# Recurrent layer: gate products in three rounded passes, the convolution's sum and the decay's square in banks, the gate weights' rest on GpSimd

## What is computed

```
xb, g = split(h @ w_in)                          # h: 512 x 1024, w_in: 1024 x 3072
xc = conv_b + conv_w[3]*xb + sum over k<3 of conv_w[k] * (xb delayed by 3-k tokens)
r = sigmoid(xc_head @ gate_a_w[head] + gate_a_b) # per head, 128 x 128
i = sigmoid(xc_head @ gate_x_w[head] + gate_x_b)
a = exp(-8 * r * softplus(-lam));  mult = sqrt(1 - a*a)
h_t = a_t * h_(t-1) + mult_t * i_t * xc_t        # scan over the tokens
y = h * silu(g);  out = y @ w_out                # w_out: 1536 x 1024
```

## Time and profile before

| | |
|---|---|
| median of 3 runs | 1899.43 us (1898.32 to 1899.71) |
| profiled execution | 1898.7 us, of which the span of its instructions is 1897.0 us |
| TensorE busy | 1859.6 us of the span (98%) |
| GpSimd, VectorE, ScalarE busy | 1323.5 us (70%), 863.7 us (46%), 476.6 us (25%) |
| mean granted TensorE clock | 0.995 of full |
| stretch 389 to 552 us, which holds the changed stage | TensorE busy 162.1 of 163.0 us |

### The profile page before, as it was taken

How to read it: one execution, slowest core, us unless ns; L and a number is a source line. 1 busy time by engine, 2 the same in 40 slices (tenths; PEclk the granted TensorE clock), 3 DMA queues, 4 the chain that set the end, 5 groups by cost and what they waited for, 6 DMA issues and landing times.

```text
span 1897.0 us, 25309 instructions
## 1 busy us (share of the span) xinstructions
PE 1859.6 (98%) x8668; PEld 1512.5 (80%) x8668; DVE 863.7 (46%) x1465; ACT 476.6 (25%) x868; POOL 1323.5 (70%) x1303
## 2 busy tenths in 40 slices
PE   7999999999999999999999999999999999999998
PEld 6888888877778788888888767798876768888886
DVE  5166663168973422233047655644354172222621
ACT  3111111146651111111033244343323231111001
POOL 7766666767677777776677887672772667777765
PEclk9999999999999999999999999999999989999999
DMA  4222224232222322232232211100331222223231
GB/s 180 92 88 89 90 91 149 90 122 75 74 83 102 112 108 88 96 128 92 83 111 100 75 59 45 45 23 1 134 111 45 70 75 97 102 88 105 95 107 71
DMA packets 25128, 170.45 MB, mean 90 GB/s; under 512 B 2784, under 2 KB 2912, under 8 KB 6624
## 3 DMA queue, kind: packets, MB, share of 16 engines
q1 hardware_dynamic: 23328, 159.92, 23.9%
q10 hardware_dynamic: 1728, 9.58, 1.4%
HBM read 167.39 MB, written 2.10 MB: 89 GB/s over the span
## 4 chain that ended last, share of the span: by engine, by line
PE 93%; DVE 3%; ACT 1%; POOL 1%; issue 1%; DMA 0%; DVEq 0%; ACTq 0%; POOLq 0%
PE bank L399 20%; PE bank L401 20%; PE bank L400 20%; PE bank L437 2%; PE bank L439 2%; PE bank L438 2%; PE bank L1219 2%; PE bank L1218 2%; PE bank L1220 2%; PE bank L786 1%; PE bank L1605 1%; PE bank L1607 1%; PE bank L1606 1%; PE bank L2264 1%; PE bank L2248 1%; PE bank L1843 1%
## 5 line engine op out<-in xcount | busy, mean ns | idle before, releaser
L303 POOL TENSOR_TENSOR weights_lo<-raw_weights,weights_hi 128x512 fp32r<-128x512 f32 (+3 forms) x560 | 759.0, 1356 | 53.1 <-ACT weights_hi L322 7.2
L301 POOL TENSOR_SCALAR weights_hi<-raw_weights 128x512 fp32r<-128x512 f32 (+4 forms) x536 | 363.7, 679 | 396.5 <-PE bank L401 281.3
L399 PE MATMUL bank<-x_hi,weights_hi 128*128 128x512 f32 x1264 | 500.3, 396 | 0.2
L401 PE MATMUL bank<-x_lo,weights_hi 128*128 128x512 f32 x1264 | 492.2, 389 | 0.0
L400 PE MATMUL bank<-x_hi,weights_lo 128*128 128x512 f32 x1264 | 491.9, 389 | 0.0
L399 PEld LDWEIGHTS bank<-x_hi,weights_hi 128*128 128x128 f32 x1264 | 237.4, 188 | 52.8 <-issue 4.3
L400 PEld LDWEIGHTS bank<-x_hi,weights_lo 128*128 128x128 f32 x1264 | 237.4, 188 | 51.9 <-issue 3.6
L401 PEld LDWEIGHTS bank<-x_lo,weights_hi 128*128 128x128 f32 x1264 | 237.3, 188 | 49.8
L1046 DVE TENSOR_TENSOR temps<-bank,rms_rows 128x512 f32<-128x512 f32 x44 | 30.4, 690 | 185.7 <-PE bank L401 185.7
L1036 ACT ACTIVATE ffn_y_hi<-temps 128x512 f32 (+1 forms) x44 | 27.8, 633 | 228.8 <-DVE temps L1049 228.8
L437 PE MATMUL bank<-weights_hi,x_hi 128*128 128x512 f32 x160 | 64.4, 402 | 11.2 <-DVE x_lo L527 10.7
(11 more groups left out here) (453 smaller groups left out, 3247.1 us busy)
## 6 DMA issues: line engine op xcount, KB each, us to landing
raw_weights<-in_ffn_up SPq DMA_DIRECT2D x44, 1024.0 KB, 4.8
raw_weights<-in_a_ug SPq DMA_DIRECT2D x16, 1024.0 KB, 4.7
raw_weights<-in_b_in SPq DMA_DIRECT2D x12, 1024.0 KB, 4.8
raw_weights<-in_ffn_down SPq DMA_DIRECT2D x8, 1408.0 KB, 6.0
raw_weights<-in_ffn_down SPq DMA_DIRECT2D x11, 1024.0 KB, 4.8
raw_weights<-in_a_out SPq DMA_DIRECT2D x8, 1024.0 KB, 4.7
raw_weights<-in_a_v SPq DMA_DIRECT2D x7, 1024.0 KB, 4.8
raw_weights<-in_b_out SPq DMA_DIRECT2D x8, 768.0 KB, 4.2
```

Of the source, the lines that this page charges most:

```text
L301: nc.gpsimd.tensor_scalar(hi, raw, 1.0, 0.0, ALU.mult, ALU.add).then_inc(S("units_hi"), 1)
L303: nc.gpsimd.tensor_tensor(lo, raw, hi.bitcast(F32), ALU.subtract).then_inc(units_ready, 1)
L399: nc.tensor.matmul(ps, wh, xh[:, k, :], start=k == 0, stop=False)
L401: last = nc.tensor.matmul(ps, wh, xl[:, k, :], start=False, stop=k == last_k)
```

## The change

The gate products become three matmuls each, as in `feature_tile`, from rounded halves. ScalarE's copy of the gate matrices is now the rounded half (`b_gate_hi`); GpSimd makes its rest (`b_gate_lo`, the new function `pool_gates_low`, called behind unit 1 of each following round, and once behind the last round). The convolution's sum stays in its bank; ScalarE copies it rounded to `b_xc_hi`, and VectorE makes the rest `b_xc_lo` (`conv_low`). The square of the decay goes to bank 4 in place of a buffer, so `gates` also waits for `b_m2`, the last read of that bank.

```diff
--- before.py
+++ after.py
@@ -153,9 +153,9 @@
     _members("sq", ("gl", 2 * GH), ("go", GH)) + [("go_act_diags", 2)], _members("sums", ("gl", GH), ("go", GH)), *(_members(kind, ("gl", GH), ("go", GH)) for kind in ("diags", "spread", "scaled")),
     *([(f"b_{b}", n * KB), (f"g_{g}", n * 3 * GH)] for b, g, n in (("xb", "xb", 1), ("xc0", "c0", 1), ("taps", "taps", 2), ("xc", "conv", 1))),
     *(_members(kind, ("fx", FOXH * TOK), ("ma", MH * TOK)) for kind in ("s", "nm", "e", "p", "t", "pt")),
-    [("row_sel", 3), ("f_rows", 1), ("gb_split", 4), ("go_with_q", TOK)], [("row_ones", 3), ("mask_b", 2), ("f_queries", 2)],
+    [("b_xc_lo", KB), ("row_sel", 3), ("f_rows", 1), ("gb_split", 4), ("go_with_q", TOK)], [("b_xc_hi", KB), ("row_ones", 3), ("mask_b", 2), ("f_queries", 2)],
     [("beta_tanh", 1), ("a_exp", 1), ("rows_exp", 1)],
-    [("causal", 2), ("masks", 26)], [("b_thg", KB), ("g_th", 4 * GH)], [("b_sg", KB), ("fx_r", FOXH * TOK)],
+    [("b_gates_lo", KB), ("causal", 2), ("masks", 26)], [("b_thg", KB), ("g_th", 4 * GH)], [("b_sg", KB), ("fx_r", FOXH * TOK)],
     [("raw_first0", 16), ("mem_in", 32)], [("raw_first1", 16), ("stored", 16 * KD)],
     [("fx_o", FOXH), ("ma_o", 2 * MH)], [("fx_hi", FOXH // 2), ("ma_hi", 2 * MH)], [("fx_lo", FOXH // 2), ("ma_lo", 2 * MH)],
 ]
@@ -257,9 +257,11 @@
         B_YH = place("b_y_hi", YAT, [KB, SEQ], F32R)
         B_YL = place("b_y_lo", YAT + 24, [KB, SEQ], F32R)
         B_GW = place("b_gate_w", YAT + 48, [KB, 2, P])
-        B_ST = place("b_gate_stage", YAT + 60, [2, 2, P])
+        B_ST = place("b_gate_hi", YAT + 60, [2, 2, P], F32R)
+        B_STL = place("b_gate_lo", YAT + 76.5, [2, 2, P], F32R)
         B_XB = place("b_xb", YAT + 62, [2, SEQ + 8])
-        B_XC = place("b_xc", YAT + 66.5, [2, SEQ])
+        B_XCH = place("b_xc_hi", YAT + 66.5, [2, SEQ], F32R)
+        B_XCL = place("b_xc_lo", 192, [2, SEQ], F32R)
         B_TG = place("b_tg", YAT + 70.5, [2, SEQ])
         B_TMP = place("b_temps", YAT + 74.5, [10, SEQ])
 
@@ -357,6 +359,8 @@
                         if very_first:
                             pool.wait_ge(*due(f"raw_first{j}", 16))
                         split_unit(pool, ph, r, j, parity)
+                        if ph.name == "b_in" and j == 1 and not first(r):
+                            pool_gates_low(pool, r - 1, 1 - parity)
                     if first(r) and after_first:
                         after_first()
                 if ph.name == "a_v":
@@ -370,6 +374,12 @@
                         body(r, r % 2, r // 2)
                 else:
                     rounds(pool, ph, body)
+                if ph.name == "b_in":
+                    pool_gates_low(pool, KB - 1, 1)
+
+        def pool_gates_low(pool, r, parity):
+            pool.wait_ge(*due("b_stage", r + 1))
+            nc.gpsimd.tensor_tensor(B_STL[:, parity, :, :], B_GW[:, r, :, :], B_ST[:, parity, :, :].bitcast(F32), ALU.subtract).then_inc(S("b_gates_lo"), 1)
 
 
         def pool_mix_out(pool):
@@ -778,12 +788,15 @@
         def pe_b_in(pe):
             def gates(r, parity):
 
-                pe.wait_ge(*due("b_xc", r + 1))
-                pe.wait_ge(*due("b_stage", r + 1))
+                pe.wait_ge(*due("b_gates_lo", r + 1))
+                pe.wait_ge(*due("b_xc_lo", r + 1))
                 if not first(r):
                     pe.wait_ge(*due("b_thi", r))
+                    pe.wait_ge(*due("b_m2", r))
                 for g in range(2):
-                    nc.tensor.matmul(PS[4 + g], B_ST[:, parity, g, :], B_XC[:, parity, :], start=True, stop=True).then_inc(S("b_gates"), 1)
+                    nc.tensor.matmul(PS[4 + g], B_ST[:, parity, g, :], B_XCH[:, parity, :], start=True, stop=False)
+                    nc.tensor.matmul(PS[4 + g], B_STL[:, parity, g, :], B_XCH[:, parity, :], start=False, stop=False)
+                    nc.tensor.matmul(PS[4 + g], B_ST[:, parity, g, :], B_XCL[:, parity, :], start=False, stop=True).then_inc(S("b_gates"), 1)
 
             def body(r, parity, pair):
                 if first(r):
@@ -825,7 +838,7 @@
                 nc.scalar.activation(A_OF[parity], TR_, ACT.Exp, scale=N4[:, bass.ds(r, 1)], bias=N4[:, bass.ds(r, 1)]).then_inc(S("b_a"), 1)
                 nc.scalar.activation(TL_, TR_, ACT.Tanh, scale=P4[:, bass.ds(r, 1)], bias=P4[:, bass.ds(r, 1)]).then_inc(S("b_tl"), 1)
                 wait(act, *due("b_a", r + 1))
-                nc.scalar.activation(A2_, A_OF[parity], ACT.Square).then_inc(S("b_a2"), 1)
+                nc.scalar.activation(PS[4], A_OF[parity], ACT.Square).then_inc(S("b_a2"), 1)
 
             def round_y(r):
                 wait(act, *due("b_y", r + 1))
@@ -856,6 +869,9 @@
                     gate_activations(r - 1, 1 - parity)
                     if not (isinstance(r, int) and r == 1):
                         round_y(r - 2)
+                wait(act, *due("b_xc", r + 1))
+                nc.scalar.activation(B_XCH[:, parity, :], PS[6 + parity], ACT.Copy).then_inc(S("b_xc_hi"), 1)
+                if not first(r):
                     side_and_root(r - 1, 1 - parity)
             rounds(act, PB, body)
             last = PB.rounds - 1
@@ -876,7 +892,7 @@
                 dve.wait_ge(*due("b_xc0", r + 1))
                 for tap in range(3):
                     tapped = nc.vector.scalar_tensor_tensor(
-                        out=B_XC[:, parity, :] if tap == 2 else PS[6 + parity], in0=B_XB[:, parity, XB0 - 3 + tap:XB0 - 3 + tap + SEQ],
+                        out=PS[6 + parity], in0=B_XB[:, parity, XB0 - 3 + tap:XB0 - 3 + tap + SEQ],
                         scalar=V_[:, bass.ds(VEC["conv"] + tap * KB + r, 1)], in1=PS[6 + parity], op0=ALU.mult, op1=ALU.add)
                     if tap < 2:
                         tapped.then_inc(S("b_taps"), 1)
@@ -898,11 +914,15 @@
 
             def input_term(r, parity):
                 dve.wait_ge(*due("b_thi", r + 1))
-                nc.vector.scalar_tensor_tensor(out=BT_, in0=TI_, scalar=1.0, in1=B_XC[:, parity, :], op0=ALU.add, op1=ALU.mult).then_inc(S("b_ix"), 1)
+                nc.vector.scalar_tensor_tensor(out=BT_, in0=TI_, scalar=1.0, in1=PS[6 + parity], op0=ALU.add, op1=ALU.mult).then_inc(S("b_ix"), 1)
+
+            def conv_low(r, parity):
+                dve.wait_ge(*due("b_xc_hi", r + 1))
+                nc.vector.tensor_tensor(B_XCL[:, parity, :], PS[6 + parity], B_XCH[:, parity, :].bitcast(F32), ALU.subtract).then_inc(S("b_xc_lo"), 1)
 
             def root_term(r):
                 dve.wait_ge(*due("b_a2", r + 1))
-                nc.vector.scalar_tensor_tensor(out=A2_, in0=A2_, scalar=1.0, in1=TL_, op0=ALU.add, op1=ALU.mult).then_inc(S("b_m2"), 1)
+                nc.vector.scalar_tensor_tensor(out=A2_, in0=PS[4], scalar=1.0, in1=TL_, op0=ALU.add, op1=ALU.mult).then_inc(S("b_m2"), 1)
 
             def low_y(r):
                 dve.wait_ge(*due("b_yh", r + 1))
@@ -929,6 +949,8 @@
                     input_term(r - 1, 1 - parity)
                     if not second:
                         low_y(r - 2)
+                conv_low(r, parity)
+                if not first(r):
                     root_term(r - 1)
                     side_gate(r - 1, 1 - parity)
 
```

## The result

| | |
|---|---|
| before | 1898.49 us (1897.57 to 1899.71, 10 runs) |
| changed | 1903.99 us (1902.40 to 1908.28, 10 runs) |
| ratio | 1.0032, 95% interval 1.0024 to 1.0040 |
| profiled execution of the changed kernel | 1903.69 us, span 1902.0 us (before, 1898.7 and 1897.0) |

The change makes the kernel 5.5 us slower. I had forecast 8.05 more.

What follows compares the result with a forecast made beforehand. TensorE's issue was taken to bound the kernel (busy 98% of the span). -4.6 + 5.7 + 1.0 + 3.15 + 1.5 + 1.3 = +8.05 us on 1898.7 gave 1906.8 us, 8-in-10 range 1901.8 to 1910.0.

Steps and rivals of the forecast that it cites:

- The saving: Gate products of twelve heads on TensorE: six rounded matmuls replace two fp32 ones, rounds 12.25 for 12.65, saving 4.6 us.
- The wait on GpSimd in round 1: GpSimd stands 11.4 us for ScalarE's copy of head 0's gate matrices; TensorE stalls 5.7 us ahead of unit (1,2).
- Rival (b): Head 0's gate-matrix copy is ready before GpSimd comes to it, so the kernel gets faster, at most 4.8 us; chance 0.05.
- The gate products of head 1: They wait for the root's term of head 0, behind conv_low on VectorE: a TensorE stall of 1.0 us.
- Middle rounds and the price of the root's term: Nothing waits in the middle rounds; the root's term, with a bank input, takes 0.75 us.
- Rival (c): Middle rounds wait too, if conv_low and the root's term cost 1.77 each: +3 to +10 us over ten rounds; chance 0.07.
- The gate products of head 11: Directly behind round 11, they wait for VectorE's root's term of head 10: a TensorE stall of 3.15 us.
- Rival (a): Only the stalls of round 1 come, the stage's end is covered: 1901 to 1902.3 us, within 0.2%; chance 0.12.
- So nothing is won back behind it: Behind the stall ahead of head 11's gate products: head 11's chain isn't late, so no time is regained.
- The clock: TensorE's clock falls to the 1.2 GHz level after both long stalls, costing 1.5 us, then likely 1.3 us.
- rival (d): As forecast, but the clock does not fall a second time, or not at all: 1904 to 1905.5; 0.76 together with the forecast.
- the sentence that neither stall ends at its own length: Stalls of 5.7 and 3.15 us each bring extra low-clock time, since the throttled level is default and activity releases it.

Runs made afterwards that it cites:

- Experiment 8: Experiment 3 with the gate products as two full fp32 matmuls per head, from the rounded halves alone: 1899.48 us, ratio 1.0007.
- Experiment 1: Changed kernel with GpSimd's rest of head 0's gate matrices moved behind unit (1,3) in place of unit (1,1): 1898.63 us, ratio 1.0000.
- experiment 5: Changed kernel with the square of the decay back in its SBUF buffer and gates not waiting for b_m2: 1905.53 us, ratio 1.0038.
- experiment 2: Changed kernel with the last head's gate products moved into b_out, behind units (0,0) and (0,1): 1902.58 us, ratio 1.0022.
- experiment 3: Changed kernel with the edits of experiment 1 and experiment 2 together: 1896.08 us, ratio 0.9987.
- experiment 9: The changed kernel again, unedited, for a second profile and more times: 1903.99 us, ratio 1.0031.
- experiment 10: Changed kernel with 13 rounded matmuls into bank 0 ahead of the last gate products, filling only that wait: 1903.85 us, ratio 1.0030.
- experiment 4: Changed kernel with 24 rounded matmuls of no use behind the spread, filling the wait of round 1: 1904.09 us, ratio 1.0031.
- experiment 7: Experiment 4 plus 13 rounded matmuls into bank 0 ahead of the last gate products, so both waits are filled: 1902.10 us, ratio 1.0019.

## Why the prediction was right in kind and 3 us too high

*The saving* (4.6, from rounds of 12.25): rounds of 12.24, and 4.8 left over in the account, at the end of its range of 4.3 to 4.8. Right. Experiment 8 puts the rounds back to 12.65 by the passes alone.

*The wait on GpSimd in round 1* (5.7, idle of 11.4): 5.7 and 11.48, at the place named. The new operation took 0.72 where I had put 0.74 between two sizes. Experiment 1 shows it as the cause: with the call moved, the idle is gone and the time is that of the kernel before. That it agrees to a tenth is partly luck: the price of the new operation was read halfway between two others. Rival (b), that ScalarE's copy would be there in time, is out by this row.

*The gate products of head 1* (1.0): 0.83. Right, with the same releaser. In experiment 1, where neither stall nor low clock holds TensorE up ahead of head 0, it is 1.2.

*Middle rounds and the price of the root's term* (no wait, 0.75): no wait, and 0.67 in all twelve rounds. Rival (c) is out. That a bank input does it was only half the reason: experiment 5 has it at 0.8 with both inputs in SBUF. The Trainium skill (SBUF — State Buffer, SBUF: two separate sides) says that the loser at the shared ports waits for the whole instruction of the other; by that a different moment can be as good as a different source. The trace agrees so far: the same form took a median of 1.77 in its old place and 0.80 in the new one, and the next instruction of the kind, the side gate, got slower.

*The gate products of head 11* (3.15): 3.1, behind the four operations named (input term, rest of y, `conv_low`, root's term). Rival (a) is out.

*"So nothing is won back behind it"*: failed. I looked only at the chain of head 11. GpSimd, for which TensorE had waited twice in `b_out` before (0.9, in the second view of waits above), uses the wait to run ahead, and 1.0 comes back (1.4 less 0.4 by the late starts). Experiments 2 and 3 show it from the other side: without the last wait TensorE stands idle for 1.3 on GpSimd there, with it 0.2.

*The clock* (1.5 behind the first stall, 1.3 behind the last): the first cost 2.0 (1.7 in experiment 9), above the 1.9 that I had as its most, and the second nothing. The second is the largest error, rival (d); the sentence that neither stall ends at its own length held for the first alone. The two errors partly cancel, which is luck. Experiments 9 and 10 speak against chance: a second profile has no fall there either, and filling that stall changes nothing in the median. The experiments also show that the rule I used, one fall for each long wait, is not one: in experiments 1 and 4, where the first low stretch is gone, the same wait of 2.88 is followed by one, and in experiment 5, where the first low stretch is there, a wait of 2.2 (2.5 by the late start) is. What decides it I can't say. It may be when the wait falls and not how long it is, but no run moves the wait alone.

The sum by measured terms is -4.8 + 5.7 + 2.0 + 0.8 + 3.1 - 1.0 = +5.8 within the stage, where the forecast has +8.05. The -4.8 in it was left over from the same account; with the 4.9 of the rounds the sum is +5.7. The 0.8 that is still between this and the 5.0 lies outside it, 0.66 of it in the first microseconds of the program, where the profiled executions differ by themselves. Open is why two of the first ten runs took 1908.1 and 1908.3 us. Their mean granted clock is 0.994, but another of the ten had 0.994 with 1902.4. Six more runs in experiment 9 had none such.

## What to carry to other kernels

A cheaper instruction mix on the engine that bounds the kernel is worth its pitch times its count, and this is easily read from two rows; what it costs is decided where the steady order breaks off, at the first and the last round, so follow each new wait there through every queue that stands behind it. Put a new step of a helper engine behind the work that the bounding engine needs next: here one call two units later was worth 5.4 us, and with the last gate products moved too the change came out 2.5 us ahead. Before a wait is priced or taken away, look for the engine that catches up during it, since part of the wait comes back elsewhere, as 1.4 of 3.1 us did.

## What the runs showed of the hardware that I had not expected

A wait of 2.88 us on TensorE was followed by a stretch at the 1.2 GHz level in experiments 1 and 4 and by none in the changed kernel, twice. With the first low stretch removed, one came at the next wait (experiment 4: gone at 403, there in 526 to 545), so that filling one wait won nothing and filling both (experiment 7) 1.9 us.

Low stretches also stand far behind the stage, and they move from profile to profile. In 1390 to 1400 the granted clock was 1.00 in the first profile of the changed kernel and 0.83 in the second (experiment 9); in 1500 to 1530 it was 0.83 in the kernel before, 0.94 in the changed one and 0.84 in experiment 2. I had taken them for a possible microsecond between two kernels. The timelines say otherwise: from the first `feature_tile` of `b_out` to the last matmul TensorE takes 1330.1 us in the kernel before, 1330.0 in the changed one and 1329.6 to 1330.2 in the ten others. TensorE waits for VectorE soon behind these stretches, and what the clock takes makes that wait shorter (1.39 and 0.50 us in the two rows of experiment 2). In these kernels a low clock cost time only in the stage, where no such wait stands behind it.

GpSimd's new operation of 128 x 256 took 0.72 us in round 1 and up to 1.54 in other rounds (722/1056/1535 ns, min, median and max of twelve), and VectorE's side gate, with two inputs in SBUF, 0.68 to 1.59. It cost nothing here, as GpSimd has a gap in these rounds, but a price read in round 1 would have been wrong for the others by a factor of two.
